# Sums of squares for the later norms of a two-layer trunk: GpSimd adds seven blocks up, TensorE sums twice

## The chip, the cores and the metric

One core of a Trainium2 chip. The metric is the device time of the whole program in microseconds (us); lower is better. The engines are TensorE (PE in the rows, PEld its weight loads), VectorE (DVE), ScalarE (ACT), GpSimd (POOL) and SyncE (SP), which issues the DMAs.

## The reference

Two decoder layers over T = 272 tokens (16 meta tokens and 256 of the input) of width 1024, in float32. Each layer does

```python
u = rmsnorm(h, attn_norm[layer])
# three token mixers (MLA, GLA, HGRN2) on u @ w_in, each with its own gate
h = h + mixed @ w_out[layer]
u = rmsnorm(h, ffn_norm[layer])
h = h + (swiglu(u) if layer % 2 == 0 else moe_swiglu(u))
```

and `rmsnorm(x, g)` is `x * rsqrt(mean(x * x) + EPS) * g`, the mean over the 1024 features. There are four such norms: before and after the mixers in layer 0, and the same in layer 1. In layer 1 the channel mixer sends each token to two of eight experts.

## The kernel before, in words

**Layout.** The residual stream lies transposed in SBUF as `hT`, 128 partitions x 8 blocks x 272 tokens: feature 128 k + p is partition p of block k. A sum over features is therefore a sum over the 8 blocks and over the partitions. TensorE does both with matmuls against a 128x128 matrix of ones (`ones`), which leave in every partition of `bank[2]` the sum over the partitions; eight of them accumulate over the blocks. `gt` (128 x 8 x 272) holds the squares, and at other times gates of the HGRN2 branch.

**Stream of jobs.** All weight products are a list of jobs (`jobs`, built at L146 and used by every engine in the same order). A job is one weight tile of 128x1024 (512 KB, `raw`), which SyncE loads six jobs ahead (`RAW` = 6, L489), ScalarE rounds to its high part `hi` (L569, `LOOK` = 3 jobs ahead), and VectorE subtracts to the low part `lo` (L841, `LOOK_LO` = 2 jobs ahead). TensorE makes three matmuls for each of the tile's k blocks (L1369 to L1371: high x high, low activation x high weight, high activation x low weight). A full tile has 24 of them. Its result goes to `bank[0]` or `bank[1]` in turn, and ScalarE or VectorE takes it out. The attention and linear attention work between the products is spread over job slots by a table (`shares`).

The kinds of jobs that matter here: `wo` (output products of the branches; for two of the three branches GpSimd adds the gated results up at L543), then eight `wout` (one block m of the 1024 outputs each), then in layer 0 `fg` and `fu` (22 pairs) and 24 `fd` (three jobs j = 0, 1, 2 with 8, 8 and 6 k blocks for each block m). After `wout` m, or `fd` 3m + 2, VectorE adds the result to block m of `hT` (L910). In layer 1 after the last `wout` comes the expert part: the router, and then for each item of 128 slots 42 chunks of 1 MB of expert weights. In layer 1 the `wo`, `wout` and some other products have only the 256 columns that are needed (`live`).

**The squares.** `squares_at` (L451 to L458) says that at job g + 1, the job behind the one that finished block m < 7, that block is squared and summed: ScalarE squares it at the start of job g + 1 (L577, which waits for L910), and TensorE sums it at the end of the same job, after its second half (L1364, called from L1584). Block 7 is squared and summed in `norm` itself. So the sum of block m stands in TensorE's order behind the products of the next job. With `wout` the next job is block m + 1, and the sum of block 6 stands behind the last product of the stretch. With `fd` the next job is the first of three of block m + 1.

**The norm.** Before the job of the next stage, `norm(phase)` runs on three engines. TensorE sums block 7 (L1364) and signals `norm_sum`. ScalarE takes the logarithm (L584) and the exponential (L586) for the reciprocal root `rr`, VectorE scales the blocks (L849), ScalarE and VectorE split them into `UH` (L589) and `UL` (L854), and TensorE's next product waits for those. Phase 0 is the norm ahead of everything; phases 1 (after `wout` of layer 0), 2 (after `fd`) and 3 (after `wout` of layer 1) are the later three.

**GpSimd.** Its only work in the loop over jobs is the adds of L543 for `wo` jobs of two branches. After the loop it clears three tiles when the last norm's `rr` is made (L546 to L548), and later three buffers (L553).

Of the kernel before, what the change touches and what calls it, by code (L numbers as in the profile page):

```python
# [19 lines left out]
ALU = mybir.AluOpType  # L20
# [5 lines left out]
KD = D // P  # L26
META = 16
SEQ = 256
T = META + SEQ
# [57 lines left out]
def live(layer, kind):  # L87

    return slice(META if layer == DEPTH - 1 and kind in ("gate", "r", "hg", "wo", "wout") else 0, T)
# [64 lines left out]
def build_schedule():  # L154


    jobs = []
    side = {}
    for layer in range(DEPTH):
        g0 = len(jobs)  # L160
        lj = layer_jobs(layer)
        kinds = [(k, i) for _, k, i in lj]
        jobs += lj
        mla = mla_steps(layer)


        at = 2 * (g0 + kinds.index(("kr", 0))) + 2
        end = 2 * (g0 + kinds.index(("wo", 11))) + 1
        heads = [s for s in mla if s[1] != "ot"]
        for n, s in enumerate(heads):  # L170
            side.setdefault(at + n * (end - at) // len(heads), []).append(s)
        for s in mla[len(heads):]:
            side.setdefault(end + s[2] // 2, []).append(s)

        for unit, first in enumerate((("gd", 0), ("f", 0), ("f", 2))):
            for s, n in la_steps(layer, unit):
                side.setdefault(2 * (g0 + kinds.index(first)) + n, []).append(s)
        if layer % 2 == 0:
            jobs += ff_jobs(layer)

    order = [(slot, s) for slot in sorted(side) for s in side[slot]]
    shares = dict(pe={}, act={}, dve={})
    for slot, s in order:
        for engine, late in zip(shares, (0, *LATE.get(s[1], (0, 0)))):
            shares[engine].setdefault(slot + late, []).append(s)
    return jobs, shares


def bass_hybrid_trunk(nc, A, out):
    jobs, shares = build_schedule()  # L190
# [17 lines left out]
    def J(layer, kind, i):  # L208
        return of_job[place[(layer, kind, i)]]
# [24 lines left out]
    def mixed_by(layer, b, m):  # L234

        return 16 * layer + 8 * (ORDER[b] - 1) + m + 1
# [4 lines left out]
    with ExitStack() as ctx:  # L241
        def sb(name, shape, dt=F32, c=ctx):
            return c.enter_context(nc.sbuf_tensor(name, shape, dt))

        def sem(name):
            return ctx.enter_context(nc.semaphore(name))

        bank = [ctx.enter_context(nc.psum_tensor(f"bank{i}", [P, 512], F32)) for i in range(8)]
# [12 lines left out]
        def gate_of(b, m):  # L261
            return (O[:, m // 4, m % 4, :], mixed[:, m, :], gt[:, m, :])[b]
# [6 lines left out]
        ident, ones = C[:, cc["ident"]], C[:, cc["ones"]]  # L269
# [4 lines left out]
        gt = sb("gt", [P, KD, T], c=mix)  # L274
# [88 lines left out]
            sem("meta_landed"), sem("const_landed"), sem("par_landed"), sem("small_landed"))  # L363
        x_landed = [sem(f"x_landed{i}") for i in range(2)]
        small_used = sem("small_used")
        zeroed = sem("zeroed")
        hi_made, lo_made = sem("hi_made"), sem("lo_made")
        stream_done = sem("stream_done")
        bank_free = [sem("bank0_free"), sem("bank1_free")]
# [1 line left out]
        norm_sq, norm_sum, norm_r, u_ready = sem("norm_sq"), sem("norm_sum"), sem("norm_r"), sem("u_ready")  # L371
# [38 lines left out]
        def drained(eng, o):  # L410

            eng.wait_ge(bank_free[o % 2], o // 2 + 1)
# [31 lines left out]
        last_out = of_job[-1]["out"]  # L444

        norm_before = {g for g, (_, k, i) in enumerate(jobs) if g and i == 0 and k in ("dq", "fg")}
        norm_after = {n + 1: of_job[g]["out"] - KD for n, g in enumerate(sorted(norm_before))}
        norm_after[len(norm_before) + 1] = last_out + 1 - KD


        squares_at = {}  # L451
        phase = 0
        for g, (_, kind, i) in enumerate(jobs):
            if kind == "wout" or kind == "fd" and i % 3 == 2:
                m = i if kind == "wout" else i // 3
                phase += m == 0
                if m < KD - 1:
                    squares_at[g + 1] = (phase, m)  # L458

        need_u = {g: n for n, g in enumerate(g for g, (_, k, i) in enumerate(jobs)  # L460
                                             if i == 0 and k in ("dq", "wout", "fg"))}
        block = ctx.enter_context(nc.Block())
# [65 lines left out]
        @block.gpsimd  # L528
        def _(pool):


            for layer, kind, i in jobs:
                if kind == "wo" and ORDER[i // 4] > 0:
                    for half in range(2):
                        b, m = i // 4, 2 * (i % 4) + half
                        o = J(layer, kind, i)["out"] + half

                        drained(pool, o)
                        drained(pool, J(layer, "wo", 4 + i % 4)["out"] + half)
                        if ORDER[b] == 2:  # L540
                            pool.wait_ge(mix_done, mixed_by(layer, 2, m))
                        c = live(layer, kind)
                        pool.tensor_tensor(mixed[:, m, c], mixed[:, m, c], gate_of(b, m)[:, c], ALU.add).then_inc(mix_done, 1)  # L543

            pool.wait_ge(norm_r, len(norm_before) + 2)
            pool.memset(ysh[:].bitcast(F32), 0.0)  # L546
            pool.memset(ysl[:].bitcast(F32), 0.0)
            pool.memset(selT[:].bitcast(F32), 0.0).then_inc(zeroed, 1)  # L548
            pool.wait_ge(items_ready, 2)
            n_before = pool.value_load(nit_i[0:1, 1:2], min_val=0, max_val=11)  # L550
            for k in range(MLOOK - 1):
                pool.wait_ge(chunk_done, n_before * ITEM + (ITEM + k - MRAW + 1))
                pool.memset(mraw[k % MRAW][:], 0.0).then_inc(mlanded[k % MRAW], 16)  # L553
# [796 lines left out]
        def _(pe):  # L1350
            MM, TR = pe.matmul, pe.transpose

            def norm(phase):

                for k in range(KD) if phase == 0 else (KD - 1,):
                    if phase == 0 and k == 0:

                        pe.wait_ge(h_loaded, KD)
                    ins = sum_squares(phase, k)
                ins.then_inc(norm_sum, 1)  # L1360

            def sum_squares(phase, m):
                pe.wait_ge(norm_sq, KD * phase + m + 1)
                return MM(bank[2][:, 0:T], ones, gt[:, m, :], start=m == 0, stop=m == KD - 1)  # L1364

# [196 lines left out]
            for k in range(KD):  # L1562
                if k % 4 == 0:
                    pe.wait_ge(x_landed[k // 4], 16)
                if k >= 2:
# [5 lines left out]
                   ident[0:META, 0:META]).then_inc(x_turned, 1)  # L1571
            pe.wait_ge(zeroed, 1)
            norm(0)

            pe.wait_ge(const_landed, 16)
            phase = 1
            for g in range(NG):
                if g in norm_before:
                    norm(phase)
                    phase += 1  # L1580
                for half in range(2):
                    stream(g, half)
                    if half == 1 and g in squares_at:
                        sum_squares(*squares_at[g])  # L1584
                    for s in shares["pe"].get(2 * g + half, ()):
                        if s[1] in PE_PART:
                            (mla if s[1] in MLA_NAMES else la)(*s)


            norm(phase)  # L1590
            pe.wait_ge(moe_const, 48)
            for k in range(KD):
# [47 lines left out]
            with nc.Fori(0, n_items, engines=bass.OrderedEngineSet([pe.engine]), hint_back_edge=True) as i:  # L1640
                for k in range(ITEM):
                    pe.wait_ge(mhi_made, i * ITEM + (k + 1))
                    h, l = mhi[k % MHI], mlo[k % MRAW]
                    if k < GU:
                        j, up, half = k // 4, k // 2 % 2, k % 2
# [15 lines left out]
                    else:  # L1661
# [13 lines left out]
                        for f in range(2):  # L1675
                            for n in range(2):
                                c = slice(f * D + n * 512, f * D + (n + 1) * 512)
                                ins = MM(bank[2 + n][:], hh[:, 2 * d + f, :], l[:, c],  # L1678
                                         start=False, stop=d == N_DN - 1 and f == 1)
# [109 lines left out]
```

## Time and profile before

| | us |
|---|---|
| median of 3 runs | 2020.01 |
| lowest and highest | 2013.38 and 2024.51 |
| the profiled execution's own time | 2015.61 |
| its span, first to last instruction | 2013.7 |
| TensorE, busy | 1962.8 |
| VectorE, busy | 1529.0 |
| ScalarE, busy | 1291.1 |
| GpSimd, busy | 40.9 |

The trace is of one execution, and times in it count from the start of its span. In the rows, "x" and a number is how many instructions a row has. A row of a timeline gives the start, the duration (of the merged instructions together, where there are several), the engine, the line, the output and inputs, and in brackets how long the engine was idle before it and what released it. Matmuls are pipelined, so that their durations overlap, and their starts say more than their durations. The mean granted TensorE clock of the whole execution was 0.983 of full speed (1.00 is 2.4 GHz, 0.50 is 1.2 GHz). The time of an execution goes roughly half to the two layers' streams of jobs and half, from about 1003 us on, to the expert items, of which each takes some 124 us.

### The profile page before, as it was taken

The page shows a single profiled execution, that of the slowest core. Times are in us where ns is not written, and L with a number is a line of the kernel's source. Part 1 is how long each engine was busy: PE and PEld are TensorE (multiplying, and loading weights), DVE is VectorE, ACT ScalarE, POOL GpSimd, SP SyncE. Part 2 cuts the span into 40 slices and gives each one's busy share as a digit, 9 for nine tenths or more (in the row PEclk, how much of TensorE's full clock was granted, in tenths as well). Part 3 has the DMA queues.
Part 4 walks back from the last instruction along what each step waited for, and adds up shares of the span by engine and source line. Part 5 has one row for each costly group of instructions (what it writes and reads, how often), then busy time and mean ns, then how long its engine had stood idle before and what let it go on. Part 6 is the DMA issues. An engine that isn't in the chain of part 4 may idle for free.

```text
span 2013.7 us, 30970 instructions
## 1 busy us (share of the span) xinstructions
PE 1962.8 (97%) x11460; PEld 1697.7 (84%) x11460; DVE 1529.0 (76%) x1872; ACT 1291.1 (64%) x1544; POOL 40.9 (2%) x42
## 2 busy tenths in 40 slices
PE   7999999999998999999899999999999999999998
PEld 6888888999997888888788888888888888888886
DVE  4848675655544858776589898998989989898897
ACT  4757474444335657666477776777777777776775
POOL 0000000200000000002000000000000000000001
PEclk9999998999999999999999999999999999999999
DMA  6424342545565424334589898998999989999994
GB/s 184 122 74 113 87 116 84 147 142 173 164 171 145 124 75 128 102 96 126 183 305 370 334 369 351 352 370 333 369 350 353 371 334 364 354 348 351 354 368 175
DMA packets 268823, 474.78 MB, mean 236 GB/s; under 512 B 10512, under 2 KB 223792, under 8 KB 225728
## 3 DMA queue, kind: packets, MB, share of 16 engines
q1 hardware_dynamic: 268736, 473.59, 67.1%
q8 instruction: 58, 0.95, 0.2%
q14 instruction: 29, 0.24, 0.0%
HBM read 472.51 MB, written 1.05 MB: 235 GB/s over the span
## 4 chain that ended last, share of the span: by engine, by line
PE 86%; DVE 5%; ACT 4%; issue 4%; POOL 0%; DMA 0%; DVEq 0%; ACTq 0%; SPq 0%; POOLq 0%
PE bank L1369 11%; PE bank L1371 10%; PE bank L1370 10%; PE bank L1655 8%; PE bank L1656 8%; PE bank L1660 8%; PE bank L1672 5%; PE bank L1678 5%; PE bank L1673 5%; DVE mlo L1166 2%; PE bank L1624 1%; PE bank L1554 1%; PE bank L1553 1%; PE bank L1687 1%; PE bank L1364 1%
## 5 line engine op out<-in xcount | busy, mean ns | idle before, releaser
L1166 DVE TENSOR_TENSOR mlo<-mraw,mhi 128x2048 fp32r<-128x2048 f32 x283 | 642.3, 2288 | 71.3 <-ACT mhi L775 70.3
L775 ACT ACTIVATE mhi<-mraw 128x2048 fp32r<-128x2048 f32 x283 | 539.6, 1915 | 103.6 <-PE bank L1660 53.0
L1369 PE MATMUL bank<-UH,hi 128*128 128x272 f32 (+1 forms) x1392 | 429.1, 308 | 13.0 <-DVE UL L854 8.6
L1371 PE MATMUL bank<-UH,lo 128*128 128x272 f32 (+1 forms) x1392 | 406.6, 292 | 0.0
L1370 PE MATMUL bank<-UL,hi 128*128 128x272 f32 (+1 forms) x1392 | 405.3, 291 | 0.0
L569 ACT ACTIVATE hi<-raw 128x1024 fp32r<-128x1024 f32 (+1 forms) x222 | 231.7, 1044 | 123.9 <-PE bank L1371 123.8
L1655 PE MATMUL bank<-mhi,xh 128*128 128x512 f32 x768 | 303.8, 396 | 2.2 <-DVE xl L1251 2.2
L1656 PE MATMUL bank<-mhi,xl 128*128 128x512 f32 x768 | 300.3, 391 | 0.0
L1369 PEld LDWEIGHTS bank<-UH,hi 128*128 128x128 f32 x1392 | 269.0, 193 | 29.3 <-issue 21.3
L841 DVE TENSOR_TENSOR lo<-raw,hi 128x1024 fp32r<-128x1024 f32 (+1 forms) x222 | 268.5, 1222 | 32.2 <-ACT hi L569 31.8
L1370 PEld LDWEIGHTS bank<-UL,hi 128*128 128x128 f32 x1392 | 269.9, 194 | 2.0 <-issue 0.5
L1371 PEld LDWEIGHTS bank<-UH,lo 128*128 128x128 f32 x1392 | 269.2, 193 | 0.0
L1660 PE MATMUL bank<-mlo,xh 128*128 128x512 f32 x896 | 240.5, 390 | 0.0
L1660 PEld LDWEIGHTS bank<-mlo,xh 128*128 128x128 f32 x896 | 168.7, 188 | 36.0
L1655 PEld LDWEIGHTS bank<-mhi,xh 128*128 128x128 f32 x768 | 144.6, 188 | 31.5 <-issue 2.3
L1656 PEld LDWEIGHTS bank<-mhi,xl 128*128 128x128 f32 x768 | 144.7, 188 | 29.3
L1166 DVE TENSOR_TENSOR mlo<-mraw,mhi_last 128x2048 fp32r<-128x2048 f32 x56 | 128.1, 2287 | 16.8 <-ACT mhi_last L775 16.6
L1672 PE MATMUL bank<-mhi,hh 128*128 128x512 f32 x352 | 137.8, 391 | 0.0
L1673 PE MATMUL bank<-mhi,hl 128*128 128x512 f32 x352 | 137.1, 389 | 0.0
L1678 PE MATMUL bank<-mlo,hh 128*128 128x512 f32 x448 | 119.8, 389 | 0.0
L775 ACT ACTIVATE mhi_last<-mraw 128x2048 fp32r<-128x2048 f32 x56 | 107.3, 1916 | 13.6 <-PE bank L1678 8.5
L1678 PEld LDWEIGHTS bank<-mlo,hh 128*128 128x128 f32 x448 | 84.1, 188 | 17.6
(350 smaller groups left out, 2721.5 us busy)
## 6 DMA issues: line engine op xcount, KB each, us to landing
mraw<-in_w_exp SPq DMA_DIRECT2D x336, 1024.0 KB, 4.8
raw<-in_w_in SPq DMA_DIRECT2D x114, 512.0 KB, 3.8
raw<-in_w_ff_gate SPq DMA_DIRECT2D x22, 512.0 KB, 3.8
raw<-in_w_ff_up SPq DMA_DIRECT2D x22, 512.0 KB, 3.8
raw<-in_w_out SPq DMA_DIRECT2D x16, 512.0 KB, 4.0
raw<-in_w_ff_down SPq DMA_DIRECT2D x16, 512.0 KB, 3.9
raw<-in_w_gla_o SPq DMA_DIRECT2D x8, 512.0 KB, 3.4
raw<-in_w_hgrn_o SPq DMA_DIRECT2D x8, 512.0 KB, 3.4
```

The source lines that it names most:

```text
L775: A_(mhi[k % MHI][:], mraw[k % MRAW][:], ACT.Copy).then_inc(mhi_made, 1)
L841: TT(lo[g % RAW][:, 0:n], raw[g % RAW][:, 0:n], hi[g % HI][:, 0:n].bitcast(F32), ALU.subtract).then_inc(lo_made, 1)
L1166: TT(mlo[k % MRAW][:], mraw[k % MRAW][:], mhi[k % MHI][:].bitcast(F32), ALU.subtract).then_inc(mlo_made, 1)
L1369: MM(ps, h, xh_, start=first, stop=False)
L1370: MM(ps, h, xl_, start=False, stop=False)
L1371: return MM(ps, l, xh_, start=False, stop=last)
L1655: MM(ps, xh[:, kt, :], h[:, c], start=kt == 0, stop=False)
L1656: MM(ps, xl[:, kt, :], h[:, c], start=False, stop=False)
L1660: ins = MM(ps, xh[:, kt, :], l[:, c], start=False, stop=kt == KD - 1)
L1672: MM(ps, hh[:, 2 * d + f, :], h[:, c], start=d == 0 and f == 0, stop=False)
L1673: MM(ps, hl[:, 2 * d + f, :], h[:, c], start=False, stop=False)
L1678: ins = MM(bank[2 + n][:], hh[:, 2 * d + f, :], l[:, c], start=False, stop=d == N_DN - 1 and f == 1)
```

## The change

For phases 1 to 3, the squares of blocks 0 to 6 are added up by GpSimd into `gt[:, 0, :]`. At the job at which ScalarE squares block m (1 to 6), GpSimd waits for that square and, for m > 1, for its own previous add, and adds block m to block 0: six adds for each norm. TensorE no longer sums in the stream of jobs. In `norm` it waits for the sixth add, sums the added block, then sums block 7 as before. Phase 0 keeps its eight sums. ScalarE's and VectorE's programs are the same, and so are the DMAs.

```diff
--- before.py
+++ after.py
@@ -363,7 +363,7 @@
             sem("meta_landed"), sem("const_landed"), sem("par_landed"), sem("small_landed"))
         x_landed = [sem(f"x_landed{i}") for i in range(2)]
         small_used = sem("small_used")
-        zeroed = sem("zeroed")
+        zeroed, sq_added = sem("zeroed"), sem("sq_added")
         hi_made, lo_made = sem("hi_made"), sem("lo_made")
         stream_done = sem("stream_done")
         bank_free = [sem("bank0_free"), sem("bank1_free")]
@@ -529,7 +529,13 @@
         def _(pool):
 
 
-            for layer, kind, i in jobs:
+            for g, (layer, kind, i) in enumerate(jobs):
+                if g in squares_at and squares_at[g][1]:
+                    phase, m = squares_at[g]
+                    pool.wait_ge(norm_sq, KD * phase + m + 1)
+                    if m > 1:
+                        pool.wait_ge(sq_added, (KD - 2) * (phase - 1) + m - 1)
+                    pool.tensor_tensor(gt[:, 0, :], gt[:, 0, :], gt[:, m, :], ALU.add).then_inc(sq_added, 1)
                 if kind == "wo" and ORDER[i // 4] > 0:
                     for half in range(2):
                         b, m = i // 4, 2 * (i % 4) + half
@@ -1352,7 +1358,7 @@
 
             def norm(phase):
 
-                for k in range(KD) if phase == 0 else (KD - 1,):
+                for k in range(KD) if phase == 0 else (KD - 2, KD - 1):
                     if phase == 0 and k == 0:
 
                         pe.wait_ge(h_loaded, KD)
@@ -1360,6 +1366,9 @@
                 ins.then_inc(norm_sum, 1)
 
             def sum_squares(phase, m):
+                if phase and m < KD - 1:
+                    pe.wait_ge(sq_added, (KD - 2) * phase)
+                    return MM(bank[2][:, 0:T], ones, gt[:, 0, :], start=True, stop=False)
                 pe.wait_ge(norm_sq, KD * phase + m + 1)
                 return MM(bank[2][:, 0:T], ones, gt[:, m, :], start=m == 0, stop=m == KD - 1)
 
@@ -1580,8 +1589,6 @@
                     phase += 1
                 for half in range(2):
                     stream(g, half)
-                    if half == 1 and g in squares_at:
-                        sum_squares(*squares_at[g])
                     for s in shares["pe"].get(2 * g + half, ()):
                         if s[1] in PE_PART:
                             (mla if s[1] in MLA_NAMES else la)(*s)
```

## Rows read from the trace of the kernel before

**Rows 1.** The page: busy us (share of the span) and instructions of each engine.

```profile
PE 1962.8 (97%) x11460; PEld 1697.7 (84%) x11460; DVE 1529.0 (76%) x1872; ACT 1291.1 (64%) x1544; POOL 40.9 (2%) x42
```

**Rows 2.** The page: the chain that ended last, by engine.

```profile
PE 86%; DVE 5%; ACT 4%; issue 4%; POOL 0%; DMA 0%; DVEq 0%; ACTq 0%; SPq 0%; POOLq 0%
```

**Rows 3.** Windows: length, busy PE, PEld, DVE, ACT, POOL; PEclk, DMA share, GB/s.

```profile
379.00:403.00 24.00, 24.00 (x183) 23.52 (x182) 11.01 (x14) 9.66 (x14) 0.00 (x0) 1.00 0.54 154
546.00:615.40 69.40, 69.40 (x542) 68.62 (x542) 28.74 (x31) 25.14 (x30) 0.00 (x0) 1.00 0.57 161
960.00:982.50 22.50, 22.50 (x182) 22.01 (x181) 8.63 (x12) 6.81 (x11) 0.00 (x0) 1.00 0.93 330
1234.00:1358.00 124.00, 123.55 (x575) 102.42 (x574) 110.49 (x77) 91.76 (x62) 0.00 (x0) 1.00 0.92 355
```

**Rows 4.** Line L1364, the sums of squares: duration in ns, first and last start.

```profile
L1364 PE MATMUL bank<-gt,C x64: 390/391/791, 13.6 to 983.8; 128*128 128x272 f32 x64
```

**Rows 5.** Timeline of TensorE around one sum in layer 0's w_out.

```profile
385.37 0.29 PE L1371 MATMUL bank<-UH,lo 128*128 128x272 f32 x1
385.49 0.62 PE L1364 MATMUL bank<-gt,C 128*128 128x272 f32 x2
...
386.07 0.28 PE L1370 MATMUL bank<-UL,hi 128*128 128x272 f32 x1
```

**Rows 6.** Timeline of VectorE in layer 0's w_out.

```profile
379.19 0.44 DVE L910 TENSOR_TENSOR hT<-hT,bank 128x272 f32<-128x272 f32 x1 [0.73 <-PE bank L1371]
...
382.21 0.44 DVE L910 TENSOR_TENSOR hT<-hT,bank 128x272 f32<-128x272 f32 x1 [1.45 <-PE bank L1371]
...
385.69 0.44 DVE L910 TENSOR_TENSOR hT<-hT,bank 128x272 f32<-128x272 f32 x1 [1.91 <-PE bank L1371]
...
399.97 1.22 DVE L841 TENSOR_TENSOR lo<-raw,hi 128x1024 fp32r<-128x1024 f32 x1
```

**Rows 7.** Timeline of TensorE around one sum in w_ff_down.

```profile
557.20 0.29 PE L1371 MATMUL bank<-HH,lo 128*128 128x272 f32 x1
...
557.92 0.28 PE L1370 MATMUL bank<-HL,hi 128*128 128x272 f32 x1
```

**Rows 8.** Timeline of VectorE in layer 1's w_out.

```profile
960.07 0.42 DVE L910 TENSOR_TENSOR hT<-hT,bank 128x256 f32<-128x256 f32 x1 [0.71 <-PE bank L1371]
...
962.88 0.42 DVE L910 TENSOR_TENSOR hT<-hT,bank 128x256 f32<-128x256 f32 x1 [1.25 <-PE bank L1371]
...
966.16 0.42 DVE L910 TENSOR_TENSOR hT<-hT,bank 128x256 f32<-128x256 f32 x1 [1.73 <-PE bank L1371]
```

**Rows 9.** Timeline of TensorE at the end of w_out (layer 0) and of w_ff_down.

```profile
402.89 0.62 PE L1364 MATMUL bank<-gt,C 128*128 128x272 f32 x2
404.58 0.72 PE L1364 MATMUL bank<-gt,C 128*128 128x272 f32 x2 [1.07 <-ACT gt L577]
...
618.35 0.73 PE L1364 MATMUL bank<-gt,C 128*128 128x272 f32 x2 [2.95 <-ACT gt L577]
```

**Rows 10.** Timeline of GpSimd in layer 0.

```profile
344.46 0.75 POOL L543 TENSOR_TENSOR mixed<-mixed,gt 128x272 f32<-128x272 f32 x1
...
364.31 1.69 POOL L543 TENSOR_TENSOR mixed<-mixed,O 128x272 f32<-128x272 f32 x1 [0.74 <-DVE O L906]
```

**Rows 11.** Timeline of ScalarE at the end of layer 0's w_out.

```profile
400.64 0.41 ACT L577 ACTIVATE gt<-hT 128x272 f32<-128x272 f32 x1
...
404.12 0.41 ACT L577 ACTIVATE gt<-hT 128x272 f32<-128x272 f32 x1
```

**Rows 12.** Timeline of VectorE: one L841 beside GpSimd adds.

```profile
367.54 1.67 DVE L841 TENSOR_TENSOR lo<-raw,hi 128x1024 fp32r<-128x1024 f32 x1
```

**Rows 13.** Timeline of VectorE in w_ff_down.

```profile
563.24 0.44 DVE L910 TENSOR_TENSOR hT<-hT,bank 128x272 f32<-128x272 f32 x1 [3.33 <-PE bank L1371]
```

**Rows 14.** Windows (columns as in rows 3): the same mixer jobs in both layers.

```profile
39.30:341.50 302.20, 299.60 (x2018) 261.29 (x2017) 202.62 (x429) 189.89 (x393) 0.02 (x1) 0.95 0.37 100
637.90:924.00 286.10, 282.87 (x2017) 245.62 (x2016) 201.87 (x429) 187.50 (x393) 0.02 (x1) 0.99 0.39 105
```


## The prediction

> **What bounds the kernel now.** I read the page's busy table first, then its chain of waits, then the windows of the stages that the change touches, then single instructions. The page gives TensorE 97% of the span and GpSimd 2% [rows 1], and the chain that ended last is 86% TensorE [rows 2]. The reader should not stop there: a share of the whole does not say that the three stretches with the sums are TensorE's. The windows do [rows 3]: in the eight w_out products of layer 0 (379 to 403 us), the w_ff_down products (546 to 615.4) and the w_out products of layer 1 (960 to 982.5) TensorE is busy for the whole of each window, at a granted clock of 1.00, with VectorE busy for 38 to 46% and ScalarE for 30 to 40% of it. An expert item after them (1234 to 1358) is 99.6% TensorE too, so what is gained ahead of it is not handed back to the DMA queue there, though its DMA share is 0.92.
>
> **What one sum costs.** A sum of squares is an L1364 matmul that the profile shows as two records, x64 for 32 sums [rows 4]. Its 0.62 us of busy time overlaps its neighbours, so I take the cost from starts. In layer 0's w_out stretch the 24 matmuls of a tile take 3.02 us [rows 6], so they start every 0.126 us; L1371 starts at 385.37 and the L1370 that would have started at 385.62 starts at 386.07 [rows 5]: 0.45 us. The period of a tile says the same: h is updated (L910) at 379.19 and 382.21 with no sum between, 3.02 us, and from 382.21 to 385.69 with one, 3.48 us [rows 6]: 0.46. In w_ff_down L1371 at 557.20 would be followed by L1370 at 557.45, and it comes at 557.92 [rows 7]: 0.47 us. In layer 1, with 256 columns in the products but 272 still in the sum, the period goes from 2.81 to 3.28 us [rows 8]: 0.47.
>
> **What is removed, and how many count.** Each of three norms loses six of eight sums, 18 in all. But where they stand matters, not the number. In layer 0's w_out the sums of blocks 0 to 5 stand between tiles; that of block 6 starts at 402.89, behind the last product, and then TensorE idles 1.07 us for ScalarE's square of block 7 [rows 9]. It is hidden now and stays so. Layer 1 has the same order. In w_ff_down a square is summed one job after its block, so all seven stand between products, and TensorE then idles 2.95 us before the last sum [rows 9]. The change lets the one remaining early sum go into that idle time. So 6 + 7 + 6 = 19 sums leave the path though only 18 are removed: 6 x 0.46 + 7 x 0.47 + 6 x 0.47 = 8.9 us; by the shifts of starts alone (0.45, 0.47, 0.45) it is 8.7. I take 8.8. If the sum moved into w_ff_down's idle time showed after all, it would be 8.3.
>
> **What is added, and what covers it.** GpSimd gets six adds of 128x272 per norm. It does the same shape at L543 in 0.75 us undisturbed, and in 1.69 us beside work of VectorE [rows 10]. The two wo loops of L543 lie ahead of w_out, so nothing is queued behind the adds on GpSimd but the memsets after the last norm, which wait for norm_r anyway. Who waits for the adds is TensorE alone, in norm(), and only for the sixth. In layer 0 ScalarE squares block 6 from 400.64 to 401.05 [rows 11]. The add then ends at about 401.85, at the worst 402.8. The last product is out by 402.89 now; with shorter tiles w_out 7 ends 3.02 us after w_out 6, at 402.45 on the same scale, and the early sum is only needed before block 7's square, now ready at 404.53 [rows 11], 404.1 on that scale. Less 0.5 us for that sum, 0.8 us are left at the worst price and 1.7 at the usual one. In w_ff_down the sixth add has two more jobs. I cost the adds at nothing; if the cover were gone, the tail of one add, 0.8 to 1.7 us, would show in each of two norms, 1.6 to 3.4 us in all. The chain of adds within a norm (0.8 us each against a period of 3.02) never backs up. The waits that GpSimd gains hold back nothing else, and TensorE's wait on sq_added only has the last sum and the next stage behind it, which wait for block 7 in any case.
>
> **The shared way into SBUF.** The trace shows that the two engines can hurt each other: L841, with two SBUF inputs, takes 1.22 us alone [rows 6] and 1.67 beside a GpSimd add [rows 12], and an add 1.69 instead of 0.75 [rows 10]. In the w_out stretches the square ends about when L841 ends (L577 at 400.64 for 0.41 us, L841 at 399.97 for 1.22), and then VectorE idles 1.9 us before each L910 [rows 6]; in w_ff_down it idles 3.33 us before L910 [rows 13]. Even 0.45 us on every L841 stays in that idle time. The Trainium skill ("SBUF — State Buffer", the section on SBUF's two separate sides) speaks against the change here: a GpSimd op that reads SBUF and a VectorE op with two SBUF inputs lock each other out for a whole instruction. By that rule each L841 or add could be held for all of the other. The times above agree that there is a price, and the idle time holds that too.
>
> **What does not shorten.** The norm's own serial stretch (square 7, last sum, Ln, Exp, then VectorE) stays. Weights: a w_out tile has to be loaded every 3.02 instead of 3.48 us. The first w_out tile shows that period already, and SyncE issues six tiles ahead. In layer 1 the transfer of the first expert chunks fills the DMA queues (share 0.93 [rows 3]), with nothing but these chunks behind the last tiles. A shorter stretch takes 2.8 us of lead from them. I cost it at nothing, since the router stands between the norm and the first expert product, and at 2.8 us if it were to show.
>
> **Sum.** Span 2013.7 - 8.8 = 2004.9 us; the profiled execution took 2015.61 us, 1.9 more than its span, so 2006.8 on its own scale. That execution is 4.4 us below the median of the runs shown, 2020.01; on the scale of the median the forecast is 2011.2 us, or 0.44% less. About 0.5% (10.1 us, so below 2009.9) is what a measurement of this kernel can tell from no change, since the three runs alone spread over 11.1 us.
>
> **Rivals.**
> (a) The granted clock in layer 1's mixers eats the gain; this one ends slower than before. The same jobs run from 39.3 to 341.5 us in layer 0 at a mean clock of 0.95 and from 637.9 to 924.0 in layer 1 at 0.99 [rows 14]. Counted as time at half clock (twice the missing share), that is 30 us against 6. The stretch is 302.2 against 286.1 us; some 30 of its tiles are 256 columns wide in layer 1, worth 0.2 us each by the periods above, about 6. The other 10 us are the clock's: 0.4 us lost for each us at 1.2 GHz. So the same work meets the lower level at very different total lengths, which also fits the spread of runs. Since the change moves all of layer 1 by 6 us, it can draw a worse pattern. If layer 1 got layer 0's, 24 x 0.4 = 10 us, the result is about 2021; it decides from some 22 us more at half clock on. For it: layer 0. Against: nothing in the change disturbs the mixers, and the earlier median already holds such draws. The other way it can give back layer 1's 6 us of low clock, 2.4 us: 2008.8, which counts as faster.
> (b) VectorE's splits are pushed onto TensorE's path by the adds: 18 x 0.45 = 8.1 us, result 2019.3. Against it is VectorE's idle time before each L910.
> (c) TensorE waits for sq_added in norm(): 1.6 to 3.4 us, result 2012.8 to 2014.6.
> (d) The change does not deliver: the tile periods stay 3.48 us because ScalarE, VectorE or a transfer takes over as the limit, result about 2020. Against it are the 3.02 us of the first tile and [rows 3].
>
> **Chances.** The forecast (adds hidden, 19 sums gone) 0.75; (a) worse draw 0.08, better draw 0.07; (b) 0.03; (c) 0.05; (d) 0.02. The forecast stands only 1.3 us above the line for "faster", and a median moves by some 3 to 5 us; so about 0.38 of its weight falls below the line, with most of the better draw: faster 0.35. Slower by over 0.5% would need 19 us more than forecast: 0.03. The rest, 0.62, is within 0.5%. Range: down to 2004.5 (a better draw, 2.4, and 4.3 of scatter) and up to 2018 ((c)'s 3.4 and 3.4 of scatter); it leaves out (b), (d) and the worse draw of (a).
>
> **What would show it.** L1364 should be x28 records (8 + 3 x 2 sums, two each). L910 should come every 3.02 us in layer 0's w_out, every 2.81 in layer 1's, and every 8.24 instead of 8.70 in w_ff_down. Eighteen GpSimd adds on gt should take 0.75 to 1.7 us each, none releasing TensorE. Between each last product and the last sum TensorE should idle as now, in w_ff_down 0.5 us less. Wrong would be: an idle stretch of TensorE before the first of the two L1364 that GpSimd ends, an L1369 released by L841, or tile periods above 3.1 us.

## The result, and the profile after

The changed kernel's median is 2006.27 us (2003.58 to 2012.45, 11 runs), the median before 2020.01 us (2013.38 to 2024.51, 11 runs). The ratio is 0.9944, 95% interval 0.9929 to 0.9959: 11.3 us less, between 8.3 and 14.3. Its profiled execution took 2006.27 us with a span of 2004.3, against 2015.61 and 2013.7: 9.4 us. The page has the lines that answer to [rows 1] and to the page's GpSimd share:

```profile
span 2004.3 us, 30931 instructions
PE 1953.7 (97%) x11424; PEld 1689.8 (84%) x11424; DVE 1529.0 (76%) x1872; ACT 1291.3 (64%) x1544; POOL 60.0 (3%) x60
```

TensorE has 36 matmul records less (18 sums of two records each), GpSimd 18 instructions more (42 to 60), and VectorE and ScalarE the same counts. The sums stand on two lines now, L1371 for the early one of the three later norms and L1373 for the others; the adds are L538. By source line (duration in ns, then first and last start in us):

```profile
L1371 PE MATMUL bank<-gt,C x6: 390/391/392, 395.0 to 974.1; 128*128 128x272 f32 x6
L1373 PE MATMUL bank<-gt,C x22: 392/402/791, 14.1 to 975.3; 128*128 128x272 f32 x22
L538 POOL TENSOR_TENSOR gt<-gt x18: 765/776/1564, 378.5 to 972.2; 128x272 f32<-128x272 f32 x18
```

Six and 22 records are the 28 that were forecast. VectorE's timeline gives the tile periods, in the three stretches in turn (L916 is the update of h, before L910; L847 the split, before L841):

```profile
377.03 0.44 DVE L916 TENSOR_TENSOR hT<-hT,bank 128x272 f32<-128x272 f32 x1 [1.45 <-PE bank L1380]
380.06 0.44 DVE L916 TENSOR_TENSOR hT<-hT,bank 128x272 f32<-128x272 f32 x1 [1.45 <-PE bank L1380]
...
546.61 0.44 DVE L916 TENSOR_TENSOR hT<-hT,bank 128x272 f32<-128x272 f32 x1 [2.88 <-PE bank L1380]
546.97 2.09 DVE L847 TENSOR_TENSOR lo<-raw,hi 128x768 fp32r<-128x768 f32 x2
...
554.86 0.44 DVE L916 TENSOR_TENSOR hT<-hT,bank 128x272 f32<-128x272 f32 x1 [2.88 <-PE bank L1380]
...
957.01 0.42 DVE L916 TENSOR_TENSOR hT<-hT,bank 128x256 f32<-128x256 f32 x1 [1.28 <-PE bank L1380]
959.86 0.42 DVE L916 TENSOR_TENSOR hT<-hT,bank 128x256 f32<-128x256 f32 x1 [1.28 <-PE bank L1380]
```

3.03, 8.25 and 2.85 us, against 3.48, 8.70 and 3.28 in [rows 6] and [rows 8] and the same way of counting for w_ff_down. VectorE still idles 1.28 to 2.88 us before each update but the first of a w_out stretch (0.71 and 0.73 us, as before). From the first to the last of the eight updates of a stretch, with their starts in brackets:

| stretch | before, us | changed, us | less |
|---|---|---|---|
| w_out, layer 0 | 23.90 (379.19 to 403.09) | 21.18 (374.01 to 395.19) | 2.72 |
| w_ff_down | 60.90 (554.54 to 615.44) | 57.73 (546.61 to 604.34) | 3.17 |
| w_out, layer 1 | 22.51 (960.07 to 982.58) | 19.88 (954.17 to 974.05) | 2.63 |
| sum | 107.31 | 98.79 | 8.52 |

The ends of the stretches, TensorE's timeline, answer to [rows 9]:

```profile
394.99 0.62 PE L1371 MATMUL bank<-gt,C 128*128 128x272 f32 x2
396.68 0.72 PE L1373 MATMUL bank<-gt,C 128*128 128x272 f32 x2 [1.07 <-ACT gt L583]
...
604.14 0.62 PE L1371 MATMUL bank<-gt,C 128*128 128x272 f32 x2
607.25 0.73 PE L1373 MATMUL bank<-gt,C 128*128 128x272 f32 x2 [2.49 <-ACT gt L583]
```

The early sum follows the last product at once, with no idle time of its own. The last sum still waits for ScalarE's square: 1.07 us as before, and 2.49 instead of 2.95 in w_ff_down, since the early sum now lies in that wait. From the last update to the logarithm it takes 2.25, 3.67 and 1.70 us, against 2.26, 3.67 and 1.70.

So 8.5 of the 9.4 us between the two traces lie in the three stretches. The mixers moved by more than that, but in opposite directions. These windows answer to [rows 14] (columns as there):

```profile
38.70:336.30 297.60, 295.20 (x2018) 257.42 (x2017) 202.63 (x429) 189.83 (x393) 0.00 (x1) 0.97 0.38 101
626.70:917.90 291.20, 288.76 (x2016) 250.52 (x2015) 201.87 (x429) 187.54 (x393) 0.00 (x0) 0.96 0.38 104
```

Layer 0, which runs before anything that was changed, took 297.6 us at a mean clock of 0.97 (before 302.2 at 0.95); layer 1 took 291.2 at 0.96 (before 286.1 at 0.99). In these two traces the differences of the clock nearly cancel, and a reader of one trace could take either for an effect of the change. Runs of either kernel also gather around two times some 7.5 us apart, and so a ratio of few runs moves with how many fall where.

### The profile page after: what moved, and what is told of

The parts are those of the page before. It is cut to its first block, busy times and chain, and to the rows that moved or that the text cites. A ratio compares the mean times of both kernels' runs of the same rounds, so it can differ in the third digit from the quotient of the medians.

```text
span 2004.3 us, 30931 instructions
## 1 busy us (share of the span) xinstructions
PE 1953.7 (97%) x11424; PEld 1689.8 (84%) x11424; DVE 1529.0 (76%) x1872; ACT 1291.3 (64%) x1544; POOL 60.0 (3%) x60
## 4 chain that ended last, share of the span: by engine, by line
PE 87%; DVE 4%; ACT 4%; issue 3%; POOL 0%; DMA 0%; DVEq 0%; ACTq 0%; SPq 0%; POOLq 0%
PE bank L1378 11%; PE bank L1380 10%; PE bank L1379 10%; PE bank L1662 8%; PE bank L1667 8%; PE bank L1663 8%; PE bank L1679 5%; PE bank L1685 5%; PE bank L1680 5%; DVE mlo L1172 2%; PE bank L1631 1%; PE bank L1563 1%; PE bank L1562 1%; PE bank L1694 1%; PE bank L1449 1%
## 5 line engine op out<-in xcount | busy, mean ns | idle before, releaser
L847 DVE TENSOR_TENSOR lo<-raw,hi 128x1024 fp32r<-128x1024 f32 (+1 forms) x222 | 268.5, 1222 | 32.3 <-ACT hi L575 31.8
```

What stands on the lines that cost most here:

```text
L847: TT(lo[g % RAW][:, 0:n], raw[g % RAW][:, 0:n], hi[g % HI][:, 0:n].bitcast(F32), ALU.subtract).then_inc(lo_made, 1)
```

## The experiments

**The changed kernel twice more.** No edit. The first set:

> The changed kernel once more, beside the kernel before. Theory (19 sums of 0.45 us leave TensorE's path, the rest of the measured 11.3 us is the granted clock's draw): the stretches between the first and last h update are 21.2, 57.7 and 19.9 us again, 8.5 us less in all, and the ratio lies between 0.993 and 0.997 (6 to 14 us). If times fall into two groups, the slower group has a mean granted clock lower by about 0.003. Rival (the change also brings a lasting better clock in the mixers): the ratio is 0.994 or below again and the mean granted clock is higher than before's.

12 runs gave a ratio of 0.9957, interval 0.9937 to 0.9976, 8.7 us. The stretches measured 21.19, 57.72 and 19.88 us. The five runs below 2008 us have a mean clock of 0.983, the seven above it 0.979. The second:

> The changed kernel, a third set. Theory: 8.5 us at an equal clock, ratio 0.9957 within 0.002. Rival (11 us as first measured): ratio 0.9945 or less and a higher mean granted clock than before's.

5 runs gave 0.9929, interval 0.9911 to 0.9946. That is outside the 0.9957 within 0.002 that was expected: the rival's number came again, with a mean clock of 0.9820 for these runs. The stretches were 21.18, 57.73 and 19.87 us. The three ratios differ although the stretches don't. Taken together, 28 runs of the changed kernel have a mean of 2008.0 us (standard error 0.7), 76 of the one before 2019.3 (0.5): 11.3 us. The mean granted clock of the 28 is 0.9811, and of the 65 runs of before that had it noted, 0.9796. Within a kernel a run is 1.63 us longer for each 0.001 of clock less, taken over all kernels of this document that ran more than once (1.77 in the changed kernel, 1.53 in the one before). So 0.0015 is 2.4 us, and brought to a clock of 0.980 the kernels take 2009.8 and 2018.7, that is 8.9 us (0.3 by the scatter of the runs). The reckoning is coarser than that 0.3: for the doubled sums below it gives 10.2 us more, where their trace's stretches show 8.7, and for ScalarE's order in the changed kernel 1.3 us less, where the traces show 2.5. Within that, the stretches account for the 8.9. Whether the change brings the better clock or whether it is drawn stays open: no run here isolates it.

**The adds alone.** The kernel before, with GpSimd's loop as in the change but its result in an unused block, while TensorE keeps all its sums:

```diff
+                    pool.tensor_tensor(mixed[:, 0, :], gt[:, 0, :], gt[:, m, :], ALU.add).then_inc(sq_added, 1)
...
             def sum_squares(phase, m):
+                if phase and m == KD - 1:
+                    pe.wait_ge(sq_added, (KD - 2) * phase)
```

> The kernel before with the 18 GpSimd adds added (their result goes to an unused block and nothing is summed from it), while TensorE keeps all its sums and waits for the sixth add before the last one. Theory: the adds cost nothing; tile periods stay 3.48, 8.70 and 3.29 us, the ratio is 1.000 within 0.002. Rival (adds hold off VectorE's L841 on TensorE's path): up to 18 x 0.45 = 8 us more, ratio 1.004, and longer periods.

The ratio is 0.9996, interval 0.9975 to 1.0017, and periods are 3.48, 8.70 and 3.28 us. VectorE's timeline of this run, in w_out and in w_ff_down:

```profile
380.10 0.44 DVE L916 TENSOR_TENSOR hT<-hT,bank 128x272 f32<-128x272 f32 x1 [1.91 <-PE bank L1379]
383.58 0.44 DVE L916 TENSOR_TENSOR hT<-hT,bank 128x272 f32<-128x272 f32 x1 [1.91 <-PE bank L1379]
...
557.14 2.09 DVE L847 TENSOR_TENSOR lo<-raw,hi 128x768 fp32r<-128x768 f32 x2
```

The same pair of splits in the kernel before, with no add:

```profile
554.90 2.09 DVE L841 TENSOR_TENSOR lo<-raw,hi 128x768 fp32r<-128x768 f32 x2
```

GpSimd's adds:

```profile
381.62 0.77 POOL L538 TENSOR_TENSOR mixed<-gt 128x272 f32<-128x272 f32 x1 [2.71 <-ACT gt L583]
558.30 1.55 POOL L538 TENSOR_TENSOR mixed<-gt 128x272 f32<-128x272 f32 x1 [162.00 <-ACT gt L583]
```

In w_out the add falls into VectorE's idle time and takes 0.77 us. In w_ff_down it meets two splits back to back, and it is GpSimd that waits, 1.55 us, while the splits take 2.09 us for two, as they do without an add at their side. The changed kernel has the same: 1.55 or 1.56 us for each of the six adds in w_ff_down, and 0.77 or 0.78 us for the twelve in the w_out stretches but one of 1.22. The adds cost no time in the stretches. Behind them the logarithm comes 2.31, 4.28 and 1.76 us after the last update, 0.05 to 0.06 us later than before apart from 0.55 us of lower clock in w_ff_down (see the delays below).

**Each early sum twice.** In the kernel before:

```diff
                         sum_squares(*squares_at[g])
+                        MM(bank[3][:, 0:T], ones, gt[:, squares_at[g][1], :], start=True, stop=True)
```

> The kernel before with each of the 21 early sums issued a second time into a bank that is not used. 19 of them lie between products, 2 behind the last product of a w_out stretch. Theory: TensorE is the limit and a sum costs 0.45 us there, so periods become 3.93, 9.15 and 3.74 us and the time grows by 19 x 0.45 = 8.6 us, ratio 1.0042; the 2 behind the last product cost nothing, since block 7's square is still awaited. Rival (a sum's cost is its 0.62 us of busy time): 11.8 us. Rival (something else is the limit): nothing.

The first to last updates are 26.67, 64.16 and 25.14 us: 2.77, 3.26 and 2.63 more, 8.66 in all, or 0.46, 0.47 and 0.44 us a sum. The ratio is 1.0035, interval 1.0016 to 1.0055 (7 us, 3 to 11). At the end of layer 0's w_out, L1585 being the doubled sum:

```profile
396.87 0.62 PE L1364 MATMUL bank<-gt,C 128*128 128x272 f32 x2
397.33 0.62 PE L1585 MATMUL bank<-gt,C 128*128 128x272 f32 x2
398.56 0.73 PE L1364 MATMUL bank<-gt,C 128*128 128x272 f32 x2 [0.61 <-ACT gt L577]
```

There the doubled sum costs nothing: the idle time falls from 1.07 to 0.61 us, and the logarithm still comes 2.25 us after the last update. Both the price of a sum and the count of 19 hold. The rival's 0.62 us a sum is out, since it asks for w_out periods of 4.10 us and they are 3.94.

**w_ff_down alone.** The change for the second of the three norms only:

```diff
+                if g in squares_at and squares_at[g][1] and squares_at[g][0] == 2:
...
+                for k in range(KD) if phase == 0 else (KD - 2, KD - 1) if phase == 2 else (KD - 1,):
...
+                if phase == 2 and m < KD - 1:
...
+                    if half == 1 and g in squares_at and squares_at[g][0] != 2:
```

> The change made for the norm after w_ff_down alone; the other two keep eight sums. Six sums are removed, but seven stood between products. Theory: period 8.25 us, first to last h update 57.7 us (before 60.9), that is 3.2 us or seven sums; TensorE's idle time before the last sum falls from 2.95 to about 2.5 us, since the early sum now stands in it. The w_out stretches stay at 23.9 and 22.5 us. Rival (only what is removed counts): 2.7 us, with the early sum's 0.45 us added between the last product and Ln.

This kernel ran once (2010.88 us), so it is read from its trace alone: 57.73 us there, 3.17 less, and 23.91 and 22.54 in the w_out stretches. TensorE's timeline:

```profile
605.48 0.62 PE L1371 MATMUL bank<-gt,C 128*128 128x272 f32 x2
608.59 0.73 PE L1373 MATMUL bank<-gt,C 128*128 128x272 f32 x2 [2.49 <-ACT gt L583]
```

Six sums are gone and seven are gained, the logarithm 3.68 us after the last update.

**How late the adds may be.** One, then three memsets ahead of the sixth add (the diff is of three):

```diff
+                    if m == KD - 2:
+                        for n in range(3):
+                            pool.memset(mixed[:, 0:4, :], 0.0).then_inc(padded, 1)
+                            pool.wait_ge(padded, 3 * (phase - 1) + n + 1)
```

> The changed kernel with one GpSimd memset of 1088 columns (about 1.0 us) before the sixth add of each of the three norms. Theory: after the sixth add the trace of the changed kernel has room for about 1.7 us in layer 0's w_out, 1.5 us in layer 1's and 8 us in w_ff_down before the early sum would push back the last one, so this costs nothing: the distance from the last h update to Ln stays 2.25, 3.67 and 1.70 us. Rival (TensorE already waits for the adds): each of the distances grows by 1.0 us.

> The same with three memsets, about 3.0 us. Theory: the room is used up in both w_out stretches, the distance grows by about 3.05 - 1.7 = 1.3 us in layer 0 and by about 1.5 us in layer 1, and stays 3.67 us in w_ff_down; 2.9 us in all, so against before still a gain of about 5.6 us, ratio 0.997. The early sum is then released by GpSimd. Rival (no wait at all comes through): 0. Rival (every one of three comes through whole): 9 us, ratio 1.000.

The kernel with one memset (1.01 us) also ran only once (2010.17 us). TensorE's timeline in layer 0 and at the end of w_ff_down:

```profile
398.54 0.29 PE L1384 MATMUL bank<-UH,lo 128*128 128x272 f32 x1
399.23 0.72 PE L1375 MATMUL bank<-gt,C 128*128 128x272 f32 x2 [0.41 <-POOL gt L542]
400.35 0.72 PE L1377 MATMUL bank<-gt,C 128*128 128x272 f32 x2 [0.39 <-ACT gt L587]
...
610.05 1.28 PE L1377 MATMUL bank<-gt,C 128*128 128x272 f32 x2 [2.49 <-ACT gt L587]
```

The early sum waits 0.41 us for GpSimd, and it costs nothing: the last sum waits for ScalarE afterwards, and the distances are 2.25, 4.22 and 1.71 us. (4.22 instead of 3.67 is not the wait. The last sum there took 1.28 us at the lower clock, and its idle time is 2.49 us as ever. The kernels with adds alone and with doubled sums had 4.28 and 4.22, and the changed kernel's own third set 3.94.) With three:

```profile
398.17 0.73 PE L1375 MATMUL bank<-gt,C 128*128 128x272 f32 x2 [2.54 <-POOL gt L542]
398.73 0.62 PE L1377 MATMUL bank<-gt,C 128*128 128x272 f32 x2
...
979.00 0.73 PE L1375 MATMUL bank<-gt,C 128*128 128x272 f32 x2 [2.17 <-POOL gt L542]
```

The add comes 3.2 us later, and the distances grow by 1.47 and 1.66 us in the two w_out stretches, expected 1.3 and 1.5; in w_ff_down TensorE waits for no add (the distance is 4.07 us, with 1.12 us of it the last sum at the lower clock). In time it is 0.9988, interval 0.9967 to 1.0009: more lost than 3.1 us would make, with a mean clock of 0.9767 over its ten runs, the lowest of all kernels here. The interval holds the expected 0.997, and the rival's 1.000 as well, so it is the trace that tells them apart. So the changed kernel's adds have 3.2 - 1.47 = 1.7 us of room in layer 0 and 3.2 - 1.66 = 1.5 us in layer 1, the size of two more adds.

**Three adds for each.** Two more of the same size ahead of each add, their result unused:

```diff
+                    for n in range(2):
+                        pool.tensor_tensor(mixed[:, 0, :], gt[:, 0, :], gt[:, m, :], ALU.add).then_inc(padded, 1)
+                        pool.wait_ge(padded, 2 * ((KD - 2) * (phase - 1) + m - 1) + n + 1)
```

> The changed kernel with each of the 18 adds preceded by two more of the same size whose result is not used. Theory: VectorE is not TensorE's limit in these stretches; L841's counterpart may take 1.7 to 2.0 us beside the adds, but the tile periods stay 3.02, 8.25 and 2.84 us and nothing is lost there. The last add ends 1.6 us later, just inside its room in layer 0 (1.7 us) and at its edge in layer 1 (1.5 us), so 0 to 0.3 us more. Rival (the shared way into SBUF reaches TensorE): 18 x 0.45 to 18 x 1.2 us, 8 to 20 us more, with longer periods.

The periods are 3.03, 8.25 and 2.84 us: VectorE never reaches TensorE. But the distance from the last update to the logarithm grows from 2.25 to 5.21 and from 1.70 to 4.43 us, 5.7 in all, not the 0 to 0.3 expected; the ratio is 0.9987, interval 0.9973 to 1.0001. Its GpSimd timeline in layer 0 and, last, in layer 1 (L539 the two extra adds, L541 the one that counts), VectorE's in layer 0 (L850 the split) and TensorE's wait in layer 0:

```profile
385.46 1.62 POOL L539 TENSOR_TENSOR mixed<-gt 128x272 f32<-128x272 f32 x2
387.16 1.64 POOL L541 TENSOR_TENSOR gt<-gt 128x272 f32<-128x272 f32 x1
388.94 2.49 POOL L539 TENSOR_TENSOR mixed<-gt 128x272 f32<-128x272 f32 x2
391.50 0.78 POOL L541 TENSOR_TENSOR gt<-gt 128x272 f32<-128x272 f32 x1
392.43 2.48 POOL L539 TENSOR_TENSOR mixed<-gt 128x272 f32<-128x272 f32 x2
394.99 0.76 POOL L541 TENSOR_TENSOR gt<-gt 128x272 f32<-128x272 f32 x1
...
974.44 1.63 POOL L539 TENSOR_TENSOR mixed<-gt 128x272 f32<-128x272 f32 x2
...
977.05 1.59 POOL L539 TENSOR_TENSOR mixed<-gt 128x272 f32<-128x272 f32 x2
```

```profile
386.46 1.71 DVE L850 TENSOR_TENSOR lo<-raw,hi 128x1024 fp32r<-128x1024 f32 x1
...
389.48 1.31 DVE L850 TENSOR_TENSOR lo<-raw,hi 128x1024 fp32r<-128x1024 f32 x1
```

```profile
399.17 0.72 PE L1374 MATMUL bank<-gt,C 128*128 128x272 f32 x2 [4.02 <-POOL gt L541]
```

I had counted 3 x 0.78 us. Beside the split, three adds take 3.5 us (388.94 to 392.43), more than the period of 3.03, so they run late by a little more with every tile. At the end of layer 1, where no split is left, three take 2.6 us (974.44 to 977.05). That is the chain backing up which the prediction excluded for one add a tile, and it is how this change would turn bad. Here the time goes through TensorE's wait for the sixth add, not through VectorE, although single splits in layer 0 grow from 1.22 us to between 1.25 and 1.77.

**ScalarE's order.** The trace of the changed kernel says what ends its last waits. At the end of layer 0's w_out and of w_ff_down ScalarE rounds the weight tile of job g + 3 (1.06 us) before it squares block 7, and at the second it also loads its function table (1.28 us). ScalarE's timeline at the end of w_ff_down:

```profile
604.40 1.06 ACT L575 ACTIVATE hi<-raw 128x1024 fp32r<-128x1024 f32 x1 [1.20 <-PE bank L1380]
605.48 1.28 ACT L762 ACT_TABLE_LOAD   x1
606.77 0.43 ACT L583 ACTIVATE gt<-hT 128x272 f32<-128x272 f32 x1
```

With the norm ahead of the rounding, in the changed kernel:

```diff
             for g in range(NG):
-                if g + LOOK < NG:
-                    split_hi(g + LOOK)
                 if g in norm_before:
                     ...
                     norm(phase)
                     phase += 1
+                if g + LOOK < NG:
+                    split_hi(g + LOOK)
```

> The changed kernel, and ScalarE does the norm (square of block 7, Ln, Exp, splits; in layer 1 the table load ahead of it) before it splits the weight tile of job g + 3, not after. Theory: TensorE's idle time before the last sum is ScalarE's order, so it falls from 1.07 to about 0.5 us in layer 0 and from 2.49 to about 0.5 us in w_ff_down; the distance from the last h update to Ln falls from 2.25 to 1.7 and from 3.67 to 1.7 us, 2.5 us in all against the changed kernel, ratio to before 0.9945 or a little lower. The early sum still finds the sixth add done. Rival (the late split of job g + 3 then holds up the next stage): no gain, and TensorE waits for hi or lo in the third job after the norm.

> The changed kernel with ScalarE's norm ahead of its weight split, once more, beside the changed kernel on the same chip. Theory: 2.5 us less between the last h updates and Ln, and a little less time at 1.2 GHz behind the shorter waits; ratio to before 0.992 to 0.9955, and 2 to 5 us below the changed kernel's mean. Rival (its first result was a lucky draw of the clock): no more than 2.5 us below.

TensorE's timeline at the two norms, and the window of 14 us from the logarithm on (columns as in [rows 3]), of the first of the two:

```profile
396.40 0.73 PE L1373 MATMUL bank<-gt,C 128*128 128x272 f32 x2 [0.53 <-ACT gt L583]
...
604.04 0.72 PE L1373 MATMUL bank<-gt,C 128*128 128x272 f32 x2 [0.53 <-ACT gt L583]
```

```profile
604.80:618.80 14.00, 11.01 (x71) 10.48 (x72) 10.27 (x23) 8.54 (x17) 0.00 (x0) 0.88 0.78 230
```

The same window of the changed kernel:

```profile
608.00:622.00 14.00, 11.17 (x73) 11.06 (x74) 10.57 (x23) 7.58 (x16) 0.00 (x0) 0.76 0.69 200
```

The distances from the last update to the logarithm are 1.72, 1.72 and 1.70 us, 0.53 + 1.95 = 2.5 us less, in both sets. Over these 14 us the granted clock is 0.88 in place of 0.76, which is half as long at 1.2 GHz, and the repeat shows 0.88 too; the run with this order alone, below, does not. The ratios to the kernel before are 0.9918 (0.9889 to 0.9948) and 0.9929 (0.9902 to 0.9956), 6 runs each. The changed kernel beside the repeat had 0.9929 as well, and means of 2004.6 and 2005.6 us, a difference of 1.0 us: the repeat's rival said no more than 2.5, so these sets don't part the two. Over all runs the means are 2003.6 us (12 runs, standard error 1.5) and 2008.0 (28 runs, 0.7). The 2.5 us are shown by the trace; that it beats the changed kernel in time is likely, and not more. The same order alone, in the kernel before:

> The kernel before with that order of ScalarE alone, all eight sums by TensorE. Theory: the two gains add up: the distances from the last h update to Ln become 1.7 us in all three norms, 0.5 + 1.95 us less than before, and periods stay 3.48, 8.70 and 3.29 us; ratio 0.9975 to 0.999. Rival (the order only helps once the sums are gone): distances as before.

Its distances are 1.72, 1.72 and 1.70 us at periods of 3.48, 8.70 and 3.29; the ratio is 0.9981, interval 0.9960 to 1.0003. In the traces the two gains are independent. Its window of 14 us from the logarithm after w_ff_down:

```profile
610.50:624.50 14.00, 11.21 (x69) 11.09 (x70) 10.06 (x23) 8.52 (x17) 0.00 (x0) 0.76 0.76 229
```

Here TensorE waited only 0.99 us before the last sum (2.95 in the kernel before), as long as the early sum's 0.46 and the wait of 0.53 together in the two sets above, and the clock is 0.76 all the same. At the norm after layer 0's w_out, with the same wait of 1.07 us, it is 0.76 over the 14 us in the changed kernel's first trace and 0.88 in its second set. So one trace each doesn't show that the shorter wait brought the better clock.

## Why the prediction was right

The forecast was 2011.2 us and 8.8 us less; the three stretches gave 8.5 us, and at an equal clock the runs give 8.9. The steps, one by one:

- **One sum costs its shift of the next product, 0.45 to 0.47 us, not its busy 0.62.** Held: by stretch the removal gave 0.45, 0.45 and 0.44 us a sum, the doubling 0.46, 0.47 and 0.44. The forecast's 8.8 against the measured 8.5 is mostly layer 1's term: 0.44 us, not 0.47. I took the period without a sum from the first tile (2.81 us), and the steady one is 2.84.
- **19 sums leave the path, not 18.** Held: w_ff_down gave seven for six, and TensorE's idle time there fell by the 0.46 us that the early sum takes.
- **The adds are hidden and nobody waits for them.** Held, with the room sized by the delays: 1.7 us in layer 0, as worked out, and 1.5 in layer 1. Rivals (b) and (c) are out, and (d) with them.
- **The shared way into SBUF.** There is a price. In w_ff_down GpSimd pays it (1.55 us an add), since the split is under way when the square is ready. Where extra adds were under way first (385.46 to 387.08), the split that started at 386.46 took 1.71 us. This agrees with the rule of the Trainium skill ("SBUF — State Buffer", its section on the two sides) that whichever of the two starts first holds the other off; the price stayed within VectorE's and GpSimd's idle time in the change itself. With three adds a tile it did not on GpSimd's side: TensorE then waited 4.02 us for the last one.
- **Rival (a), the clock's draws.** Draws of the size that it named came, in both directions: 4.6 us less in layer 0's mixers, 5.1 more in layer 1's, in the very trace of the changed kernel. They did not eat the gain. The price that I worked out, 0.4 us for each us at 1.2 GHz, agrees with the runs: 0.001 of mean clock is 2.0 us of full speed, or 4.0 us at half clock, and costs 1.63.
- **What was missed.** The median came out 4.9 us below the forecast, 13.7 us below the median before. By the reckoning at an equal clock 8.9 us are the change; 2.4 come from a mean clock 0.0015 higher, to which I had given only small chances, and the rest is how the runs of so small a sample fall around the median. How far the median lands from the forecast is in part luck: the same kernel's medians in the next two sets were 2011.10 and 2005.59 us. The first set's ratio lies past the 0.5% line, which I had at 0.35 against 0.62 for "within"; the second set's, 0.9957, doesn't.

## What to carry to other kernels

Price a removed instruction by how far it shifts the start of what follows on the bound engine, and look at where each one stands: those behind the last product, in the shadow of another engine's work, are worth nothing, and a job moved into that shadow is worth its whole price. Small work given to an idle engine is free as long as a chain of it, at its price beside its neighbour and not alone, is shorter than the period that feeds it, and the last of it ends before anyone waits. When an effect is as large as the scatter, note each run's granted clock and compare at an equal clock, and read the stage in the trace before believing the ratio.

## What the runs showed of the hardware

A float32 sum of 272 columns against a matrix of ones takes two matmul records and 0.44 to 0.47 us of TensorE at 2.4 GHz, where a product of the same shape in the rounded format takes 0.126 us. Layer 0's mixer work took 297.6 us at a mean granted clock of 0.97 and 302.2 at 0.95, layer 1's 286.1 at 0.99 and 291.2 at 0.96. A GpSimd add of 272 columns took 0.77 us by itself and 1.55 where VectorE's splits were under way, and those splits were no longer for it (2.09 us for two). In the 14 us from a norm's logarithm after w_ff_down the granted clock was 0.88 in two traces with a short wait of TensorE (0.53 us) and 0.76 in a third with 0.99 us, as it was with 2.49 and 2.95 us.
